# The first two experts run as a pair, routing in another order, one load moved, and GpSimd in the last norm

## The reference, cut to what matters

```python
x = layer_norm(ALPHA * x + mixer(x), ln1_g, ln1_b)
# route: 16 experts in 4 groups, best group, best 2 of its 4
probs = softmax(x @ w_router + b_router)
# each chosen expert, for its tokens, weighted by its gate:
f = silu(x @ w1[e]) * (x @ w3[e]) @ w2[e]        # [1024 x 1024] each
x = layer_norm(ALPHA * x + f, ln2_g, ln2_b)
...
return rms_norm(x, final_norm_g)
```

## Time and profile before

| | us |
|---|---|
| median of 3 runs (1777.67 to 1778.08) | 1777.9 |
| the profiled execution | 1778.61 |
| its span | 1777.4 |
| PE busy | 1708.9 (96%) |
| DVE, ACT, POOL busy | 790.3, 625.0, 121.9 |
| read from HBM | 542.19 MB, 306 GB/s over the span |

### The profile page before, as it was taken

One profiled execution on the slowest core, in us unless ns is written; L12 is line 12 of the kernel. 1 busy time (PEld: TensorE's weight loads), 2 busy tenths in 40 slices (PEclk: granted clock), 3 DMA queues, 4 the chain that ended last, 5 costly groups with the idle time before them and its releaser, 6 DMA issues.

```text
span 1777.4 us, 23957 instructions
## 1 busy us (share of the span) xinstructions
PE 1708.9 (96%) x10000; PEld 1114.8 (63%) x10000; DVE 790.3 (44%) x1510; ACT 625.0 (35%) x1201; POOL 121.9 (7%) x143
## 2 busy tenths in 40 slices
PE   9999999998989989999999989999999999999998
PEld 8974344433334974444343333887999899789986
DVE  6961111111103782111111012866888677668875
ACT  5541110100002661000100001666666564656664
POOL 0000000000000000000000000131111001401100
PEclk9999999999999999999999999999999999999999
DMA  9759999999999789999999999533555544335550
GB/s 392 308 226 358 403 428 428 428 429 426 426 426 419 288 320 365 429 428 429 427 429 427 425 427 419 181 140 135 176 188 182 197 166 145 141 131 174 183 190 24
DMA packets 55941, 544.90 MB, mean 307 GB/s; under 512 B 6289, under 2 KB 6289, under 8 KB 8337
## 3 DMA queue, kind: packets, MB, share of 16 engines
q1 hardware_dynamic: 55440, 542.14, 76.0%
q10 hardware_dynamic: 384, 1.13, 0.2%
HBM read 542.19 MB, written 1.05 MB: 306 GB/s over the span
## 4 chain that ended last, share of the span: by engine, by line
PE 67%; DMA 20%; DVE 7%; ACT 3%; issue 1%; POOL 1%; SPq 0%; ACTq 0%; DVEq 0%
PE PS L1208 23%; DMA ring<-in_w 20%; PE PS L410 12%; PE PS L412 11%; PE PS L411 11%; DVE wl L393 2%; PE PS L1188 2%; PE PS L1262 2%; PE PS L925 1%; ACT wh L387 1%; PE PS L1224 1%; PE PS L1276 1%; PE PS L1371 0%; DVE F L1060 0%; PE PS L1330 0%
## 5 line engine op out<-in xcount | busy, mean ns | idle before, releaser
L1208 PE MATMUL PS<-ring,F 128*64 128x512 f32 x2072 | 462.0, 595 | 28.5 <-DMA ring<-in_w 23.6
L393 DVE TENSOR_TENSOR wl<-ring,wh 128x512 fp32r<-128x512 f32 x504 | 362.9, 738 | 166.6 <-ACT wh L387 163.9
L387 ACT ACTIVATE wh<-ring 128x512 fp32r<-128x512 f32 x504 | 314.5, 630 | 271.7 <-PE PS L412 251.3
L1208 PEld LDWEIGHTS PS<-ring,F 128*64 128x64 f32 x2072 | 146.2, 137 | 322.0 <-issue 279.3
L410 PE MATMUL PS<-xh,wl 128*128 128x256 f32 x1144 | 329.7, 288 | 2.4 <-DVE wl L393 2.3
L411 PE MATMUL PS<-xl,wh 128*128 128x256 f32 x1144 | 323.5, 283 | 0.0
L412 PE MATMUL PS<-xh,wh 128*128 128x256 f32 x1144 | 323.5, 283 | 0.0
L410 PEld LDWEIGHTS PS<-xh,wl 128*128 128x128 f32 x1144 | 219.2, 192 | 5.6 <-DVE wl L393 2.4
L411 PEld LDWEIGHTS PS<-xl,wh 128*128 128x128 f32 x1144 | 219.3, 192 | 0.7
L412 PEld LDWEIGHTS PS<-xh,wh 128*128 128x128 f32 x1144 | 219.3, 192 | 0.0
L410 PE MATMUL PS<-wh,xl 128*128 128x512 f32 x352 | 142.6, 405 | 6.4 <-DVE xl L555 3.5
(11 more groups left out here) (405 smaller groups left out, 1909.5 us busy)
## 6 DMA issues: line engine op xcount, KB each, us to landing
ring<-in_w SPq DMA_DIRECT2D x100, 2048.0 KB, 25.6
ring<-in_w SPq DMA_DIRECT2D x65, 1024.0 KB, 11.4
ring<-in_ffn_up SPq DMA_DIRECT2D x44, 1024.0 KB, 4.9
early<-in_w SPq DMA_DIRECT2D x16, 2048.0 KB, 27.3
F<-in_w SPq DMA_DIRECT2D x16, 2048.0 KB, 28.6
ring<-in_ffn_down SPq DMA_DIRECT2D x22, 1024.0 KB, 4.9
F<-in_w SPq DMA_DIRECT2D x20, 1024.0 KB, 8.1
ZX<-in_w SPq DMA_DIRECT2D x8, 2048.0 KB, 28.7
```

What stands on the lines that cost most here:

```text
L387: act.e.activation(self.wh[:, p % NPIECE, :], self.piece_source(p), ACT.Copy).then_inc(*self.up("w_hi", p))
L393: dve.e.tensor_tensor(self.wl[:, p % NPIECE, :], self.piece_source(p), f32(self.wh[:, p % NPIECE, :]), ALU.subtract).then_inc(*self.up("w_ ...
L1208: t = pe.e.matmul(PS[64 * half:64 * half + 64, bank, :], lhs(k), weights[:, a:a + 512], start=(k == 0), stop=(k == 7))
```

## The change

It has four parts.

1. The first pair of experts runs together. The loads' order becomes w1 of both experts chunk by chunk, w3 of both, w2 of both (`FIRST_PAIR`), and TensorE's order: for each of four chunks two features' gathers and the w1 products of both experts, w3 of expert 0, half of w3 of expert 1, the turns of expert 0, the other half, w2 of expert 0, the gathers of the next pair with the turn of expert 1, w2 of expert 1. Each gathered feature is copied by itself.
2. Routing: block 1's second half is normalized by ScalarE; ScalarE has nine features and VectorE seven; block 1's logits go to PSUM rows 64 to 79 of another bank and alternate with block 0's; one matmul less makes the ranks.
3. The operands of the output projection after the first all lie in `xl`, and the slot of `xh` (19) is loaded once the input projection has ended, as the 16th load in layer 0 and the 13th in layer 1. ScalarE waits for the use of the second operand before it writes the fourth.
4. In the last norm GpSimd makes three of the four products with the weights, and ScalarE takes all square sums before it scales.

```diff
-FIRST_SLOTS = ([12, 13, 14, 15, XT_SLOT] + [None] * 11 + [16, None, ONCE_SLOT, None, 17, 18, 19, 20],
-               [None] * 8 + [16, XT_SLOT, 15, None, None, 14, None, 13, None, 12, ONCE_SLOT, None, 17, 18, 19, 20])
+FIRST_SLOTS = ([12, 13, 14, 15, XT_SLOT] + [None] * 10 + [19, None, 16, None, ONCE_SLOT, None, 17, 18, 20],
+               [None] * 8 + [16, XT_SLOT, 15, None, 19, None, 14, None, 13, None, 12, ONCE_SLOT, None, 17, 18, 20])
...
+FIRST_PAIR = ([12 * ex + c for c in range(4) for ex in range(2)] +
+              [12 * ex + 4 * w + c for w in (1, 2) for ex in range(2) for c in range(4)])
...
-        LOAD_ORDER[m + 7:m + at + 1] = LOAD_ORDER[m + 8:m + at + 1] + [m + 7]
+        pair = [m + i for i in FIRST_PAIR if i != 7]
+        LOAD_ORDER[m:m + 24] = pair[:at] + [m + 7] + pair[at:]
```

```diff
+        for k in range(3):
+            self.scalar_route_feature(layer, 0, k)
+        self.scalar_norm_last(ROUTED[layer])
+        self.scalar_route_feature(layer, 0, 3)
+        for k in (0, 1, 2, 3, 7):
+            self.scalar_route_feature(layer, 1, k)
...
+        for h in range(2):
+            dve.wait_ge(self.at("turned", f"route{layer}", h, 1))
+            for k in range(4, 8 - h):
+                dve.e.tensor_scalar(self.RT[:, k, h * 128:h * 128 + 128], self.turned_bank(h, k), g[:, k:k + 1],
+                                    b[:, k:k + 1], ALU.mult, ALU.add).then_inc(*self.up("xt_odd", layer, h, k))
+
+    def logits_of(self, h):
+
+        return self.PS[64 * h:64 * h + 16, 2 * h, 0:128]
...
-        self.tensor_logits(layer, 0, range(4, 8))
-        self.tensor_logits(layer, 1, range(8))
+        for i, k in enumerate((0, 1, 4, 2, 5, 6, 3, 7)):
+            if i < 5:
+                self.tensor_logits(layer, 0, i + 3)
+            self.tensor_logits(layer, 1, k)
```

```diff
+        for c in range(4):
+            for kk in range(2):
+                self.tensor_first_gather(layer, 2 * c + kk)
+            for ex in range(2):
+                n = CHUNK[f"moe{layer}"] + 12 * ex + c
...
+                    pe.wait_ge(self.first_gathered(layer, k))
+                    for half in range(2):
+                        a = kk * 1024 + half * 512
+                        t = pe.e.matmul(PS[64 * half:64 * half + 64, self.first_bank(ex, 0), :],
+                                        xg[:, k, ex * 64:ex * 64 + 64], weights[:, a:a + 512], start=(k == 0), stop=(k == 7))
+                t.then_inc(*self.up("expert_chunk", n))
...
+        self.tensor_first_product(layer)
+        pe.wait_ge(at("counts_read", layer))
+        self.tensor_product(layer, 0, 1, self.first_bank(0, 1), slots[0])
+        self.tensor_product(layer, 1, 1, self.first_bank(1, 1), slots[1], range(2))
+        self.tensor_turn_hidden(layer, 0)
+        self.tensor_turn_gates(layer, 0)
+        self.tensor_product(layer, 1, 1, self.first_bank(1, 1), slots[1], range(2, 4))
+        pe.wait_ge(at("hid_t", layer, 0))
+        self.tensor_product(layer, 0, 2, 5, hidden)
+        self.tensor_gather(layer, 1, 0)
+        self.tensor_turn_hidden(layer, 1)
+        self.tensor_gather(layer, 1, 1)
+        pe.wait_ge(at("hid_t", layer, 1), at("y0", layer, 0), at("y1", layer, 0))
+        self.tensor_product(layer, 1, 2, 5, hidden)
```

```diff
+            squares = self.F[:, 8704 + 512 * d:9216 + 512 * d] if stage == "down1" else self.Z[:, h, c]
...
-        self.scalar_split_x("ow_out", 3, GT[:, 6:8, :], at("od_join", 3))
+        self.scalar_split_x("ow_out", 3, GT[:, 6:8, :], at("od_join", 3), at("w_used", p + 7))
...
+        if layer:
+            for d in range(2):
+                self.pool_gain(0, d)
+        self.pool_rstd(0, (f"down{layer}", 0))
+        if layer:
+            self.pool_gain(1, 0)
+        self.pool_rstd(1, (f"down{layer}", 1))
...
+        self.vector_residual("down1", p, nk, 0, 1.0, self.X)
+        self.vector_rms_sum("down1", 0)
+        self.vector_residual("down1", p, nk, 1, 1.0, self.X)
+        dve.wait_ge((self.s_row, 48), at("resid", "down1", 1, 1))
+        dve.e.tensor_tensor(self.Z[:, 1, 512:1024], self.X[:, 1, 512:1024], self.last_gain()[:, 512:1024], ALU.mult
+                            ).then_inc(*up("y_gain_last"))
+        self.vector_rms_sum("down1", 1)
+        for h in range(2):
+            dve.wait_ge(at("rstd", ("down1", h)), at("y_gain_last") if h else at("y_gain", 0, 1))
             dve.e.tensor_scalar(self.Z[:, h, 512:1024], self.Z[:, h, 512:1024], self.sm[:, 500 + h:501 + h], None,
                                 ALU.mult).then_inc(*up("y_ready1", h))
```

More of the change, by code:

```diff
@@ L344, in extra_free @@
             return [self.at("od_join", 16 - slot)]
+        if slot == SPLIT_SLOTS[2]:
+            return [self.at("w_used", PIECES[mixer] - 1)]
         if slot in F_SLOTS or slot == ONCE_SLOT:
@@ L522, in tensor_out_last @@
         pe, PS = self.pe, self.PS
+        xh, xl = self.operand(stage, nk // 2 - 1)
         pe.wait_ge(self.at("g_lo", stage, nk // 2 - 1))
@@ L542, in operand @@
     def operand(self, stage, q):
+        if stage in MIXER_OUT and q:
+            a = 4 * ((q + 1) % 2)
+            return self.xl[:, a:a + 2, :], self.xl[:, a + 2:a + 4, :]
         s = slice(2 * q % 8, 2 * q % 8 + 2)
@@ L1173, in silu @@
         v = self.moe_views()
[L1174 removed]
+        return v["hh"] if ex > 1 else v["Y"][0] if ex else self.F[:, 768:1280]
     def expert_done(self, layer, ex, w):
@@ L1190, in tensor_gather, with tensor_product @@
         t.then_inc(*self.up("gathered", layer, q, half))
-    def tensor_product(self, layer, ex, w, bank, lhs):
+    def tensor_product(self, layer, ex, w, bank, lhs, chunks=range(4)):
         pe, PS = self.pe, self.PS
         swap = ex % 2 if w == 2 else 0
[L1196 to L1199, removed]
+        for c in chunks:
+            if c == 2 and w < 2:
                 pe.wait_ge(self.at("xg1", layer, ex // 2))
@@ L1302, in tensor_route_turn @@
         for d in range(2):
-            pe.wait_ge(at(f"norm{h}", stage, d), frees[h][d])
+            pe.wait_ge(at("norm1_last", stage) if h and d else at(f"norm{h}", stage, d), frees[h][d])
             for k in range(4 * d, 4 * d + 4):
@@ L1325, in tensor_logits @@
         pe = self.pe
         wr = self.col("wr").rearrange("p (k e) -> p k e", k=8)
[L1327 to L1333, removed]
+        pe.wait_ge(self.cols_in, self.route_feature(layer, h, k))
@@ L1335, in moe_tensor_route @@
+        t = pe.e.matmul(self.logits_of(h), wr[:, k, :], self.RT[:, k, h * 128:h * 128 + 128], start=k == 0, stop=k == 7)
+        if k == 7:
+            t.then_inc(*self.up("logits", layer, h))
     def moe_tensor_route(self, layer):
@@ L1375, in tensor_first_features_of @@
-    def tensor_first_features_of(self, layer, c):
-        if c in (1, 2):
-            self.tensor_first_gather(layer, c + 1)
-        self.pe.wait_ge((self.at("xg0", layer, "first"), self.at("xg1", layer, "first"), self.at("xg0", layer, 0),
-                         self.at("xg1", layer, 0))[c])
+        for h in range(2):
+            t = pe.e.matmul(self.first_gathered_of(k), self.X[:, h, k * 128:k * 128 + 128], v["S"][:, h, :],
+                            start=(h == 0), stop=(h == 1))
+        t.then_inc(*self.up("gathered", layer, 0, k))
@@ new lines, in tensor_first_pair @@
+    def tensor_first_pair(self, layer):
+        pe, at, v = self.pe, self.at, self.moe_views()
+        slots = [(lambda k, ex=ex: v["xg"][:, k, ex * 64:ex * 64 + 64]) for ex in range(2)]
+        hidden = (lambda k: v["hT"][:, k % 4 * 128 + k // 4 * 64:k % 4 * 128 + k // 4 * 64 + 64])
+        self.tensor_first_product(layer)
[12 more added lines that the diff above has]
+        self.tensor_product(layer, 1, 2, 5, hidden)
```

239 lines of the change are left out of this document (145 added, 94 removed).

## The result

| | before | after |
|---|---|---|
| median us (range, runs) | 1778.01 (1777.67 to 1778.32, 5) | 1796.93 (1795.52 to 1797.22, 5) |
| span of the profiled execution | 1777.4 | 1795.8 |

The changed kernel is slower: ratio 1.0103, 95% interval 1.0093 to 1.0114, 18.9 us by the medians and 18.4 by the spans. The forecast was 1793.8.

The account below looks back on a forecast made before the run. Both expert stages were taken to end when their last weight chunk lands, so transfers bound them. +8.5 - 1.3 + 11.1 - 1.2 - 1.2 = +15.9 us on the median 1777.9 gave 1793.8; range 1784 to 1800.

Parts of the forecast that it names:

- routing, first layer: First layer's routing: logits end at 125.85 instead of 127.18 because alternating matmuls overlap; -1.3 us, bounds 0 to 1.5 saved.
- first expert stage, from the first gather: First layer's expert stage: load 32 held back costs 11.1 us, less 2.6 the kernel before loses itself; +8.5 us.
- routing, second layer: Second layer's routing: same gain, slightly less because the first turn starts later against the rest; -1.2 us, bounds 0 to 1.5.
- second expert stage: Second layer's expert stage: loads fall 4.5 chunks behind the kernel before while load 32 waits; +11.1 us.
- last norm: Kernel's end: GpSimd makes three of four products, last scaling starts at 1772.75 not 1773.94; -1.2 us, bounds -1.7 to +0.3.
- What the loads wait for: Expert stages' load queue: load 32 waits for the seventeenth product instead of the ninth, issued 35.4 us after the first gather.
- full rate from 37.4 on: Expert stages, 37.4 us after first gather: load 32 moves, queue never empties again; slow single loads could add up to 2.5.
- the prediction's last sign: Ends of the expert stages: the prediction is wrong if the chain of waits there is TensorE; no size given.
- One more chunk early: Output projections: load 16 moved earlier only lengthens the transfers' rest before load 25; 0 us, up to 2.456 a layer otherwise.
- The queue is not held back: Rival, expert stages: loads 26 to 42 find slots in TensorE's new order; -8.3 us, 1769.6; chance 0.09.
- TensorE's stalls: Rival: TensorE stalls on copies (or single loads are slow), +1 to +4, and serial logits, +2.5; 1796 to 1800; chance 0.22.
- The queue held back for less: Rival, both expert stages: gathers and turns overlap products, load 32 comes 3 to 5 us earlier; 1783 to 1788; chance 0.12.

Follow-up runs that it names:

- the fastest version: The changed kernel with slots of a stage's first 24 chunks ranked by TensorE's order of use and loads 41 to 44 issued singly; 1769.25 us, ratio 0.995.

## Why the prediction was right, point by point

The direction, the mechanism and its place were right, and the time lay in the range, 3.1 us above the forecast. By spans the change cost 18.4 where the sum said 15.9. The terms, each read from the two profiled executions (a stage goes from its first gather to VectorE's last addition, 562.33 and 1103.50 before, 571.43 and 1122.85 after):

| term | forecast | measured |
|---|---|---|
| start of the span (first transfer lands later) | 0 | +0.3 |
| routing, first layer | -1.3 | -1.2 |
| first expert stage, from the first gather | +8.5 | +10.0 |
| routing, second layer | -1.2 | -0.9 |
| second expert stage | +11.1 | +11.1 |
| last norm | -1.2 | -1.2 |
| rest | 0 | +0.3 |
| sum | +15.9 | +18.4 |

**What the loads wait for.** The queue's times were worked out as 3.0, 7.7, 12.4 and 17.1 us after the first gather for loads 25 to 28, and 20.5, 22.3 and 24.0 for 29 to 31. They were 3.1, 7.9, 12.6, 17.4, 20.8, 22.6 and 24.3 (135.12 to 156.24, less 131.98). Load 32, forecast at 35.4, came at 35.75 in both layers. Of the nine freed slots that the prediction counted behind it eight could have taken a load; the once-used one is never given out again. The Trainium skill (DMA: Bandwidth & Descriptors, Anatomy of one DMA — SWDGE (gpsimd) path) says that a semaphore wait of a DMA happens on the sequencer that issues it, before dispatch; the rows agree, nothing behind load 32 is issued for 11.5 us.

**The first stage was under-sized by 1.5.** The step that failed is the one after the hole: I set the transfers to full rate from 37.4 on. They ran at 403 GB/s for the 14.3 us from 169.7 (the row above) against 428 later, (428 - 403)/428 x 14.3 = 0.8 us. The windows show where it lies:

```profile
169.70:176.00 6.30, 6.30 (x45) 4.06 (x42) 0.69 (x1) 1.68 (x3) 0.00 (x0) 1.00 0.99 375
176.00:184.00 8.00, 8.00 (x44) 3.31 (x44) 0.69 (x1) 0.00 (x0) 0.00 (x0) 1.00 1.01 425
```

The rate is low until about 176, when load 42 has been issued, and then full. The prediction had named this, up to 2.5, but left it out of the sum. Load 32's lateness is another 0.35; some 0.3 is left that I can't place. In the second layer the windows after the hole show 411 GB/s, (427 - 411)/427 x 14.3 = 0.5 us lost, and load 32 is as late, yet the term came out as forecast, +11.1 (the last chunk's landing moved by 19.3, less the 8.2 by which the first gather had moved). So errors of mine cancel there, and which ones was not found: that this term is exact is luck.

**What ends the stages.** I took the transfer until 1098.5 for the last chunk's. It was an earlier one's; the last chunk landed at 1101.1. In the changed kernel it landed at 1120.4, and in both kernels TensorE starts the product with it 0.5 us later. The chain from the last awaited transfer to the stage's end (1110.44 to 1122.85) is work of TensorE, VectorE and ScalarE, as it was in the first stage before (549.92 to 562.33). By the letter of the prediction's last sign that speaks against it, but each long wait ahead of it is for a transfer, so the loads still set the end.

**Routing.** The logits end at 124.45 + 2.16 = 126.61, not at 125.85, and not at 127.2 either. The step that was wrong is the price of the matmuls that alternate between row groups. I took them, from the products, as about half, and that half was itself worked out from the logits' rate and not read: no run has the products in one row group. The logits took 0.146 each where they alternate against 0.229, a third less, and the last four, which hardly alternate, 0.86 together. The features were 0.4 later than the 125.5 that I took as well: ScalarE's last one ended at 125.90 (124.05 + 1.85), 0.27 of it because the routing started later.

```profile
124.45 2.16 PE PS L1368 x26
```

The timelines of VectorE give the start of the norm's last statistics, in the kernel before and then in the changed one:

```profile
120.43 0.70 DVE L582 BATCH_NORM_STATS2 sm<-PS 128x6 f32<-128x512 f32 x1 [0.66 <-PE PS L412]
```

```profile
120.70 0.70 DVE L594 BATCH_NORM_STATS2 sm<-PS 128x6 f32<-128x512 f32 x1 [0.66 <-PE PS L420]
```

Counted from there the logits end 0.84 earlier instead of 1.3. The run with one row group had them end 6.69 after those statistics (120.27 to 126.96), close to before (6.75), so nearly all of the 0.84 is the row groups. From the logits' end to the first gather it is 5.37 in place of 5.70: the split bias add and the matmul saved in the ranks, which I had set against each other, gave 0.33. The nearly right sum in the first layer (-1.2) is thus partly luck; why the second layer gained only 0.9 was not taken apart. The Trainium skill (TensorEngine Tiling (Array Packing), Key Properties) lets tiles run in parallel; the trace agrees in part, a third less time for 16 wide outputs of 128 columns and not half, and its drain on a change of mode isn't told apart here.

**One more chunk early**: nothing, as said, and the runs with it taken back show the idle stretch in which it ends.

**Last norm**: -1.2, by a path that was wrong in places. GpSimd's three products took 1.30 (two) and 1.27, not 1.35, and they were not what ended last. The timeline of GpSimd, changed kernel (start us, us, what, idle time before it):

```profile
1786.52 2.59 POOL L3001 TENSOR_TENSOR ZX<-X,F 128x512 f32<-128x512 f32 x2 [56.47 <-DVE X L769]
1789.07 0.55 POOL L576 TENSOR_TENSOR sm<-sm,mhalf 128x1 f32<-128x1 f32 x1
1789.58 1.27 POOL L3001 TENSOR_TENSOR ZX<-X,F 128x512 f32<-128x512 f32 x1
1791.60 0.72 POOL L576 TENSOR_TENSOR sm<-sm,mhalf 128x1 f32<-128x1 f32 x1 [0.75 <-DVE sm L791]
```

It waits 0.75 for VectorE's sum of squares. The powers took 0.55 and 0.72 and not 0.94, and the product that VectorE still has (0.72) stands ahead of that sum. Slower GpSimd products would have been hidden up to 0.75 in all, and faster ones, for which the prediction named -1.7, would have gained nothing. That the sum comes out at -1.2 is partly luck: the shorter last power made up for a sum of squares that was ready 0.2 later than forecast.

**The rivals.** The queue is not held back: with the slots put right that case was run and gave 1774.66, not 1769.6; the term that I had missed is that the first double transfer then waits longer for its two slots (6.6 us of hole and not none). With single loads it is 1769.25, close to the 1769.6, but with load sizes that this rival didn't have. TensorE's stalls: none in the chain. The queue held back for less: no, 35.75 in both layers.

## What to carry to other kernels

When the order of use changes, the order in which buffers are given out must change with it: a queue that issues in order stops at the first buffer that is freed late, however many others are free behind it. Here one list that ranked slots by chunk number turned an edit worth 3 to 5 us into a loss of 19 (1777.84 without the pair, 1796.93 with it). And where loads bound a stage, the page's busy rows hide such a hole; read the gaps between issues on the load queue and the first wait in the chain that a transfer ends.

## What the runs showed of the hardware that was not expected

- Matmuls of 128 columns into 16 rows took 0.229 us each in one row group and 0.146 when they alternated between rows 0 and 64 (nine of them in 2.06 and 1.31 us): overlap gave a third. The mean over all 13, 0.226 and 0.167, shows less, since only the first nine alternate throughout.
- After a pause the transfers didn't run at full rate although the DMA share was 0.98 to 1.00. After the hole it was 375 GB/s for 6.3 us, while loads came 1.7 us apart, and 425 for the next 8, once ten had been issued. At the start of the stage it was 405 over 35 us in the fastest version and 369 over 32 us where the chunks' slots came free one by one, against 427 to 428 in the saturated stretch. A low rate goes with few loads issued ahead in all of them; whether that is the cause was not tried.
- GpSimd's power of a [128, 1] tile took 0.55, 0.72 or 0.94 us, and idling doesn't sort these times. In the norm after the first expert stage of the changed kernel it took 0.54 after 451.54 us of idling and 0.92 after 0.29 (timeline of GpSimd: start us, us, what, idle time before it); what sets it was not tried.

```profile
574.55 0.54 POOL L576 TENSOR_TENSOR sm<-sm,mhalf 128x1 f32<-128x1 f32 x1 [451.54 <-DVE sm L608]
...
575.65 0.92 POOL L576 TENSOR_TENSOR sm<-sm,mhalf 128x1 f32<-128x1 f32 x1 [0.29 <-DVE sm L572]
```
